# Seven gather buffers in place of eight, and two more weight slots of the last layer kept on chip

## The reference

```python
q = (xt @ w_q).reshape(T, PEER_HEADS, 2, PEER_HALF)        # 8 heads
s = jnp.einsum('thpe,pne->thpn', q, sub_keys)              # 128 keys per half
top_s, top_i = lax.top_k(s, PEER_TOPK)                     # 16 of each half
cand = top_s[:, :, 0, :, None] + top_s[:, :, 1, None, :]   # 256 pairs
best_s, best_j = lax.top_k(cand.reshape(...), PEER_TOPK)   # 16 experts per head
gate = jax.nn.softmax(best_s, axis=-1)
h = jnp.einsum('td,thkd->thk', xb, u[eb])                  # gathered rows of u
a = jax.nn.gelu(h, approximate=False) * gb
return jnp.einsum('thk,thkd->td', a, v[eb])                # gathered rows of v
```

## Time and profile before

| | |
|---|---|
| median of 3 runs | 2075.84 us (2075.06 to 2077.94) |
| the profiled execution | 2079.32 us, span 2077.5 us |
| PE busy | 1889.9 us (91%) |
| DVE busy | 1385.7 us (67%) |
| ACT busy | 892.3 us (43%) |
| POOL busy | 599.4 us (29%) |
| moved by all DMA queues | 712.93 MB, mean 343 GB/s |
| queue of the transfers issued by POOL (gathers among them) | 550.86 MB, 64.4% of the 16 engines' span |
| queue of the transfers issued by SP and ACT | 159.39 MB, 20.2% |

### The profile page before, as it was taken

How to read it: one execution, slowest core, us unless ns; L and a number is a source line. 1 busy time by engine, 2 the same in 40 slices (tenths; PEclk the granted TensorE clock), 3 DMA queues, 4 the chain that set the end, 5 groups by cost and what they waited for, 6 DMA issues and landing times. The chain is left out here.

```text
span 2077.5 us, 24540 instructions
## 1 busy us (share of the span) xinstructions
PE 1889.9 (91%) x7948; PEld 1177.2 (57%) x7948; DVE 1385.7 (67%) x2957; ACT 892.3 (43%) x2409; POOL 599.4 (29%) x563
## 2 busy tenths in 40 slices
PE   8999999999998989877999998879999989878776
PEld 8888678887954645432565534546665455332222
DVE  8778566666738776899534645767855566994444
ACT  5657454454633343334324623333455334343332
POOL 0002200000003444343433334333335433444331
PEclk9999999999999999999999999999999999999999
DMA  6633555544549999999999999999999999999997
GB/s 244 224 130 111 192 193 184 194 170 168 217 153 383 421 421 402 421 416 421 405 421 421 421 421 421 421 421 404 421 420 412 422 421 409 421 413 421 422 421 303
DMA packets 99915, 712.93 MB, mean 343 GB/s; under 512 B 11088, under 2 KB 11216, under 8 KB 14800
## 3 DMA queue, kind: packets, MB, share of 16 engines
q0 software_dynamic: 77040, 550.86, 64.4%
q1 hardware_dynamic: 22320, 159.39, 20.2%
q10 hardware_dynamic: 432, 1.16, 0.1%
HBM read 710.32 MB, written 1.05 MB: 342 GB/s over the span
## 5 line engine op out<-in xcount | busy, mean ns | idle before, releaser
L1436 PE MATMUL bank<-arena 128*128 128x512 f32 x2048 | 977.6, 615 | 163.7 <-ACT arena L2054 162.9
L2492 DVE SCALAR_TENSOR_TENSOR arena<-arena,x_tok 128x1024 f32<-128x1024 f32 x512 | 619.1, 1225 | 456.1 <-DMA arena<-peer_uv,arena 452.4
L2211 POOL DMA_INDIRECT arena<-peer_uv,arena x512 | 566.2, 1106 | 892.5 <-PE bank L1436 738.4
L1436 PEld LDWEIGHTS bank<-arena 128*128 128x128 f32 x2048 | 374.4, 194 | 650.6 <-issue 336.3
L2047 ACT ACTIVATE arena<-arena 128x1 f32<-128x1 f32 x512 | 103.1, 201 | 852.7 <-DVE arena L2492 852.1
L905 PEld LDWEIGHTS bank<-xT,weight_ring 128*128 128x128 f32 x1408 | 186.5, 193 | 39.0 <-issue 32.0
L2041 ACT ACTIVATE arena<-const_tile,arena 128x128 f32<-128x128 f32 x512 | 198.2, 387 | 0.0
L2054 ACT ACTIVATE arena<-arena 128x128 f32<-128x128 f32 x512 | 197.7, 386 | 0.5
L905 PE MATMUL bank<-xT,weight_ring 128*128 128x128 f32 (+1 forms) x1408 | 196.4, 293 | 0.8 <-DVE xT L2235 0.8
L905 PE MATMUL bank<-x_low_high,z_high 128*128 128x512 f32 (+1 forms) x480 | 136.5, 352 | 0.0
L1181 PE MATMUL bank<-x_split,w_split 128*128 128x512 f32 x704 | 128.7, 341 | 2.6 <-DVE x_split L2772 2.6
(11 more groups left out here) (319 smaller groups left out, 1966.9 us busy)
## 6 DMA issues: line engine op xcount, KB each, us to landing
weight_ring<-weights SPq DMA_DIRECT2D x150, 1024.0 KB, 4.9
arena<-peer_uv,arena POOLq DMA_INDIRECT x512, 14.5
row_ring<-rows_in POOLq DMA_DIRECT2D x10, 512.0 KB, 4.9
arena<-weights POOLq DMA_DIRECT2D x5, 512.0 KB, 8.5
const_tile<-consts POOLq DMA_DIRECT2D x1, 1849.0 KB, 9.2
kept_keys<-weights POOLq DMA_DIRECT2D x3, 512.0 KB, 8.7
x_tok<-x_in SPq DMA_DIRECT2D x2, 512.0 KB, 4.4
memT<-memT_in POOLq DMA_DIRECT2D x1, 1024.0 KB, 6.1
```

The source lines that it names most:

```text
L1436: ins = pe.matmul(b[:, :], diag[n % DIAGS], gbuf[n % GBUF][:, 1, h * 512:(h + 1) * 512], start=n % P == 0, stop=n % P == P - 1)
L2211: pool.indirect_dma_start(gbuf[n % GBUF].rearrange("p a d -> p (a d)"), None, peer_uv, bass.IndirectOffsetOnAxis(ap=expert[t][:, s:s + 1]. ...
L2492: dve.scalar_tensor_tensor(u, u, 1.0, x[:, t, :], ALU.mult, ALU.mult, accum_out=hdot[:, s:s + 1])\
```

## The change

The number of gather buffers goes from eight to seven. The second of the eight, columns 2048 to 4096 of `arena`, holds two weight slots of layer 1 in its place: its fourth and fifth key block. The other buffers stay where they are, so the buffer over `mixT` is now number 3. The two slots are loaded by POOL once, after `gla_intra` has been read out, behind the load of `kept_w`. They are left out of the ring's sequence for both tiles, which then has 47 slots for each. `layer_weights(i)` hands PE a kept slot or the next one of the ring.

```diff
-KEPT_KEYS = 3
+KEPT = 5
+KEPT_OWN = 3
-GBUF = 8
-MIX_BUF = 4
+GBUF = 7
+MIX_BUF = 3
...
-    layer = keys[KEPT_KEYS:] + list(v.transpose(0, 2, 1, 3).reshape(6, P, SLOT))
+    layer = keys + list(v.transpose(0, 2, 1, 3).reshape(6, P, SLOT))
     layer += slots_of_columns(q)
     layer += slots_of_rows(a["w_out_2"][1])[:NK - 2] + slots_of_columns(a["peer_w_q_2"][1])
+    layer, kept = layer[KEPT:], layer[:KEPT]
     out += layer * NT
...
+        kept = [kept_own[:, i, :] for i in range(KEPT_OWN)]
+        kept += [area(2 * D + SLOT * i, SLOT) for i in range(2)]
+        def kept_source(i):
+            return weights[n_slots - 4 - (KEPT + 1) // 2 + i // PAIR, :, i % PAIR * SLOT:(i % PAIR + 1) * SLOT]
...
-        gbuf = [area(2 * D * b, 2, D) for b in range(GBUF)]
-        lo = 2 * D * GBUF
+        gbuf = [area(2 * D * b, 2, D) for b in (0, *range(2, GBUF + 1))]
+        lo = 2 * D * (GBUF + 1)
...
+            def layer_weights(i):
+                return kept[i] if i < KEPT else next_weights()
...
-                            pe.wait_ge(sem("kept_keys_loaded"), 16 * KEPT_KEYS)
-                        kept = kept_keys[:, i, :] if i < KEPT_KEYS else None
-                        block_of((f"dil_k_{o}_{i // 4}", 0), i % 4, 4 if i < 4 else 2, tile_xT, kept=kept)
+                            pe.wait_ge(sem("kept_loaded_early"), 16 * (KEPT_OWN + 2))
+                        block_of((f"dil_k_{o}_{i // 4}", 0), i % 4, 4 if i < 4 else 2, tile_xT, w=layer_weights(i))
...
                 if r == NROW + 3:
                     wait_drained(pool, ("gla_intra", 0))
                     pool.dma_start(kept_w, weights[n_slots - 2, :, :]).then_inc(sem("kept_loaded"), 16)
+                    for i in range(KEPT_OWN, KEPT_OWN + 2):
+                        pool.dma_start(kept[i], kept_source(i)).then_inc(sem("kept_loaded_early"), 16)
```

More of the change, by code:

```diff
@@ L533, in weight_slots @@
     keys = slots_of_columns(kv[:, :768])
-    layer = keys[KEPT_KEYS:] + list(v.transpose(0, 2, 1, 3).reshape(6, P, SLOT))
+    layer = keys + list(v.transpose(0, 2, 1, 3).reshape(6, P, SLOT))
     layer += slots_of_columns(q)
     layer += slots_of_rows(a["w_out_2"][1])[:NK - 2] + slots_of_columns(a["peer_w_q_2"][1])
+    layer, kept = layer[KEPT:], layer[:KEPT]
     out += layer * NT
     out += [np.zeros((P, SLOT), np.float32)] * (len(out) % PAIR)
-    out += keys[:KEPT_KEYS] + [np.zeros((P, SLOT), np.float32)] * (KEPT_KEYS % PAIR)
+    out += kept + [np.zeros((P, SLOT), np.float32)] * (KEPT % PAIR)
     out += peer_q[:4] + slots_of_columns(bw[:, 2304:]) + slots_of_rows(a["w_out_2"][1])[NK - 2:]
@@ L632, in build @@
         rows = sb("row_ring", [P, NROW, D])
-        kept_keys = sb("kept_keys", [P, KEPT_KEYS, SLOT])
+        kept_own = sb("kept_own", [P, KEPT_OWN, SLOT])
         cst = sb("const_tile", [P, n_const])
@@ L689, in area @@
             return v
+        kept = [kept_own[:, i, :] for i in range(KEPT_OWN)]
+        kept += [area(2 * D + SLOT * i, SLOT) for i in range(2)]
+        assert len(kept) == KEPT
+        def kept_source(i):
+            return weights[n_slots - 4 - (KEPT + 1) // 2 + i // PAIR, :, i % PAIR * SLOT:(i % PAIR + 1) * SLOT]
         ident = c("ident")
@@ L1450, in add_slot, with block_of @@
                     pe.sem_inc(sem("psum_filled"), 2)
-            def block_of(key, i, n, lhs, tokens=P, kept=None):
+            def layer_weights(i):
+                return kept[i] if i < KEPT else next_weights()
+            def block_of(key, i, n, lhs, tokens=P, w=None):
                 b = begin(key) if i == 0 else bank(key)
-                w = next_weights() if kept is None else kept
+                w = next_weights() if w is None else w
                 for k in range(NK):
@@ L1464, in value_step @@
                     if part % 4 == 0:
-                        wt["values"] = next_weights()
+                        wt["values"] = layer_weights(DSLOTS + part // 4)
                     w = wt["values"]
@@ L2170, in _ @@
                 load_row(pool, n)
-            for i in range(KEPT_KEYS):
-                pool.dma_start(kept_keys[:, i, :], weights[n_slots - 6 + i // 2, :, i % 2 * SLOT:(i % 2 + 1) * SLOT])\
-                    .then_inc(sem("kept_keys_loaded"), 16)
+            for i in range(KEPT_OWN):
+                pool.dma_start(kept[i], kept_source(i)).then_inc(sem("kept_loaded_early"), 16)
             pool.wait_ge(sem("psum_filled"), ids[("att_turn", 2 * len(UNITS) - 1)] + 1)
```

## The result

The changed kernel is slower: 2083.23 us median of 20 runs (2075.78 to 2091.54) against 2076.10 us (2072.81 to 2079.86), a ratio of 1.0039 with a 95% interval of 1.0031 to 1.0048, or +8.1 us (+6.4 to +10.0). The forecast was +15.2 us. The profiled execution took 2082.98 us, with a span of 2081.2 us.

The account below looks back on a forecast made before the run. Bytes through the DMA engines were taken to bound the second half. From the profiled run, 2079.3 - 5.0 + 20.2 = 2094.5; against the median, 2075.8 + 15.2 = 2091.0 us, range 2077 to 2102.

Parts of the forecast that it names:

- The bound: Second half of the kernel: bytes through the 16 DMA engines set the time, mostly at 421 GB/s.
- The saving, 5.0 us: Layer 1's two tiles: two ring transfers of 1 MiB fewer, 2.484 us each, save at most 5.0 us.
- The moved loads and the moved wait, 0: Before and at the first gathers: loading two kept slots and waiting at gather 3 instead of 4 cost 0.
- The lost buffer, 20.2 us: Where PE and DVE run late: one queued gather fewer loses DMA time, 17.4 + 2.8 = 20.2 us.
- Seven places x 2.484 = 17.4: Seven stretches already below 421 GB/s with eight buffers: each loses a whole 2.484 us transfer, 17.4 us.
- The three near places: 650 to 700, 920 to 984 and 1775 to 1815 us, at 420 to 422 GB/s: lose 2.8 us together.
- the floor of 7.8 us in all ten places: Seven short and three near stretches: charging only the shortfall below 7.8 us from issue to landing gives 13.9 us.
- The floor of 7.8 us: Gather stream: 7.8 us, the lowest issue-to-landing time seen in sequence, taken as the least that loses nothing.
- The 12.5 near the end: Last 200 us: issue to landing at 12.5 us instead of 15.0, at unchanged 422 GB/s.
- the queue needs far less: Gather queue: a gather issued 5.1 us ahead suffices, the shorter queue never runs out; 2070.8 us, chance 0.14.
- Full price everywhere: All ten short or near stretches lose 2.484 us each; +19.8 us, 2095.7 us, chance 0.17.
- The overlap rival: Seven short stretches: late landings hold PE and DVE half the time, so the buffer costs 8.7; 2079.6 us, chance 0.12.

Follow-up runs that it names:

- e2: Kernel before with its eight gather buffers, but 47 weight-ring slots a tile instead of 49, two blocks using other slots' weights: ratio 0.9973, -5.6 us.
- e1: Kernel before with seven gather buffers instead of eight, still 49 ring slots a tile and no extra kept slots: ratio 1.0045, +9.3 us.
- e10: Repetition of the kernel with seven gather buffers and 49 ring slots a tile, against the kernel before: ratio 1.0055, +11.4 us.
- e6: Kernel before with nine gather buffers instead of eight, still 49 ring slots a tile, some blocks using the first kept slot's weights: ratio 1.0005, +1.0 us.
- e7: Kernel before with nine gather buffers for the first 126 turns, then eight; two kept slots loaded later, during the gathers: ratio 1.0017, +3.5 us.

## Why the prediction was right or wrong

The direction was right, and the time, 2083.23 us, lies in the stated range of 2077 to 2102; it lies below the forecast's own range (2084.7 to 2096), and the +15.2 us forecast are nearly twice the +8.1 measured.

*The bound.* Right: bytes through the DMA engines set the time from the first gather on; two transfers taken away or added move it by -5.6 and +5.6 us.

*The saving, 5.0 us.* Right (e2).

*The moved loads and the moved wait, 0.* Right as far as the profile goes: POOL issues the loads ahead of 29 us of idling, and the first gather is not later.

*The lost buffer, 20.2 us.* That a shorter store loses time where PE and DVE are late was right, and the size wrong; this is the step that failed. By e1 and e10 the buffer cost 9.3 and 11.4 us, by the change and e2 8.1 + 5.6 = 13.7, and by the last increments of the changed kernel and the one before 27.8 - 16.7 = 11.1. The sum had two terms. "Seven places x 2.484 = 17.4" charged a full transfer to each place that was already short; the missing transfer there rose by 3.5 us only; it rose at 1400 us (2.1 to 4.7) and 1550 us (1.3 to 2.6) and fell at 984 us (2.1 to 0.8). The three near places cost 5.0 instead of 2.8, and a stretch that was not on the list, 1430 to 1550 us, 2.6. The alternative that the prediction worked out and passed over, the floor of 7.8 us in all ten places, gave 13.9. The ground for passing it over, that the rate already falls at a minimum of 9.4 us, had a row against it: from 1775 to 1815 us the minimum is 9.4 too, and the rate 422.

What was wrong in the 17.4 was the reading of the earlier trace rows: that 11.2 us were already lost with eight buffers, and that these places were at the end of their store. The share is a mean over sixteen engines. With eight buffers, the engines that run ahead came to the end of their store and the lagging one did not, so time was not lost in step with the mean. That the missing share is not lost time is shown for the three places before 1002 us by e6, which filled them and gained nothing, and for two of them by e7. That the last engine does not run dry with eight or nine buffers and does with seven is read from its increments (16.2 to 17.7 us against 27.0 to 29.3). No run took load off that engine, so that it alone sets the time was not tested by a change.

*The floor of 7.8 us.* Too high. The seven-buffer kernel e10, from issue to landing: from 650 to 700 us, near the end (1860 to 2040 us), and over all gathers.

```profile
DMA to landing us min/median/max: 6.6/10.0/12.7
...
DMA to landing us min/median/max: 8.5/12.5/13.4
...
DMA to landing us min/median/max: 5.6/12.2/19.1
```

The 12.5 near the end is as forecast. From 650 to 700 us the minimum went from 8.7 to 6.6, by less than a transfer, and in the stream it goes down to 6.0 (at 1566 us), where the prediction said some 7; the 5.6 over all is the first gather, with nothing queued before it. Of its other signs, the missing transfer in the seven places was to reach about 28 us and is 14.7, and the last gather was to be issued about 15 us later and is issued 6.4 us later (2057.8 against 2051.4).

*The rivals.* That the queue needs far less fell with e1 and e10: the buffer costs some 10 us. The fit of the Trainium skill's page "DMA: Bandwidth & Descriptors", section "Anatomy of one DMA — SWDGE (gpsimd) path", an estimated 4.4 us for a gather, is 1.2 us short of the first gather of e10, which had nothing queued before it (5.6). It is the time of one gather, and says nothing of a store that has to outlast a late PE. Full price everywhere fell: 8.1 us, not 19.8. The overlap rival, 8.7 us for the buffer and +3.7 for the change, was nearer to the measured time than the forecast; that the lateness overlaps as it says was not shown.

## What to carry to other kernels

A buffer ring in front of a saturated DMA stream is a store of time, and its worth is not linear in its length: here the ninth buffer brought nothing, the eighth some 10 us, the seventh near 50. Before a buffer is traded for bytes (here 5 us), measure the ring one shorter and one longer; a dip in the mean DMA share does not tell on which side of the bend one stands. The last of the sixteen increments does: where it keeps the stream's pace through the dips, a further buffer has nothing to give. Here the end of the stream told the same, with a share of 0.06 for some us at eight and nine buffers and not at seven; that this holds for other kernels is not shown.

## What was not expected of the hardware

The sixteen DMA engines do not stay in step over hundreds of transfers, and the lag of the last one grows with the number of buffers: the sixteen increments of one 1 MiB gather lie 2 to 3.3 us apart with six or seven buffers, 4.3 to 5.8 with eight and 7 to 9.5 with nine, and the stream ends with 2 us or 4 us at a share of about 0.06. The last engine is not slower: where only gathers run, all sixteen take 2.48 us for each. It is set back in steps of about 1 us by instruction fetches that share it with the gathers, 16 KiB or 8 KiB each, and with eight or nine buffers it is hardly late for any other reason. Which DMA engine it is, and whose instructions those are, the trace does not say; no run moved the fetches, so what they cost the kernel, some 16 us, is an estimate from its steps.

No version was found that beats the kernel before: the saving alone (e2, 2070.63 us) has no room on chip for its two slots, and was run with other slots' weights.
